# Modulation unit 4 of an adaLN hybrid layer summed on GpSimd instead of TensorE

## What is computed

```python
mod = silu(c) @ w_ada + b_ada                  # c: 1024 values, w_ada: 1024 x 3072
shift, scale, gate = split(mod, 3)
h = layer_norm(x) * (1 + scale) + shift
xa, ga, u, v, gb = split(h @ w_in, SPLITS)     # w_in: 1024 x 2560
ya = pool_mixer(xa) * silu(ga)
yb = sgu_mixer(gelu(u), gelu(v)) * silu(gb)
y = concatenate([ya, yb]) @ w_out
out = layer_norm(2**0.25 * x + gate * y) * ln_g + ln_b
```

## Time and profile before

| | |
|---|---|
| median of 3 runs | 660.97 us (660.58 to 661.17) |
| the profiled execution, its own time | 661.66 us |
| its span, first to last instruction | 659.6 us |
| TensorE products | 647.1 us busy, 98% |
| VectorE | 497.2 us, 75% |
| ScalarE | 255.7 us, 39% |
| GpSimd | 53.0 us, 8% |
| mean granted TensorE clock | 0.998 |

### The profile page before, as it was taken

How to read it: one execution, slowest core, us unless ns; L and a number is a source line. 1 busy time by engine, 2 the same in 40 slices (tenths; PEclk the granted TensorE clock), 3 DMA queues, 4 the chain that set the end, 5 groups by cost and what they waited for, 6 DMA issues and landing times.

```text
span 659.6 us, 8435 instructions
## 1 busy us (share of the span) xinstructions
PE 647.1 (98%) x3046; PEld 540.7 (82%) x3046; DVE 497.2 (75%) x981; ACT 255.7 (39%) x340; POOL 53.0 (8%) x77
## 2 busy tenths in 40 slices
PE   7999999999999999999999999999999999999995
PEld 6888888888888888888888888888888888888885
DVE  5678897887979988499959865778968845336776
ACT  4424634346512324244655323333756333323300
POOL 2000111000002230000002210000002210000010
PEclk9999999999999999999999999999999999999999
DMA  8989776989489997957658965847558886553111
GB/s 337 380 320 373 255 278 243 325 282 350 126 315 355 405 378 242 397 196 265 215 206 316 382 216 201 312 159 257 192 177 305 289 300 205 192 170 141 41 65 64
DMA packets 52170, 168.62 MB, mean 256 GB/s; under 512 B 5477, under 2 KB 9633, under 8 KB 52130
## 3 DMA queue, kind: packets, MB, share of 16 engines
q1 hardware_dynamic: 43490, 136.63, 57.3%
q10 hardware_dynamic: 8640, 31.46, 13.6%
HBM read 139.75 MB, written 28.32 MB: 255 GB/s over the span
## 4 chain that ended last, share of the span: by engine, by line
PE 95%; DVE 2%; DMA 1%; ACT 0%; issue 0%; SPq 0%; DVEq 0%; POOL 0%
PE bank_b L1374 67%; PE bank_a L1374 23%; PE bank_a L1509 2%; DMA x_norm<-in_x 1%; PE bank_a L1492 1%; DVE w_low L865 1%; DVE v_gelu L922 0%; PE bank_b L1398 0%; DVE x_stats L896 0%; PE bank_b L1434 0%; PE bank_b L1492 0%; PE bank_b L1453 0%; PE bank_b L1425 0%; ACT h_high L712 0%; DVE z L1358 0%
## 5 line engine op out<-in xcount | busy, mean ns | idle before, releaser
L1374 PE MATMUL bank_b<-h_high,w_high 128*128 128x512 f32 x512 | 202.2, 395 | 0.2 <-DVE h_low L882 0.2
L1374 PE MATMUL bank_b<-h_high,w_low 128*128 128x512 f32 x512 | 199.5, 390 | 0.0
L1374 PE MATMUL bank_b<-h_low,w_high 128*128 128x512 f32 x512 | 199.4, 389 | 0.0
L702 ACT ACTIVATE w_high<-w_float 128x1024 fp32r<-128x1024 f32 x98 | 103.1, 1055 | 111.3 <-DMA w_float<-in_w_units 71.1
L1374 PEld LDWEIGHTS bank_b<-h_high,w_high 128*128 128x128 f32 x512 | 96.2, 188 | 20.3 <-issue 0.8
L1374 PEld LDWEIGHTS bank_b<-h_high,w_low 128*128 128x128 f32 x512 | 96.1, 188 | 20.1
L1374 PEld LDWEIGHTS bank_b<-h_low,w_high 128*128 128x128 f32 x512 | 96.2, 188 | 19.3 <-issue 0.2
L638 POOL TENSOR_TENSOR z_rstd<-z_var_eps,minus_half 128x1 f32<-128x1 f32 x16 | 20.1, 1255 | 439.9 <-DVE z_var_eps L1168 229.6
L876 DVE TENSOR_TENSOR w_low<-w_float,w_high 128x1024 fp32r<-128x1024 f32 x38 | 46.3, 1220 | 8.1 <-ACT w_high L702 7.8
L1374 PE MATMUL bank_b<-w_low,y_high 128*128 128x512 f32 x96 | 37.4, 389 | 0.0
L1374 PE MATMUL bank_a<-w_high,y_low 128*128 128x512 f32 x96 | 37.4, 389 | 0.0
(11 more groups left out here) (233 smaller groups left out, 1044.0 us busy)
## 6 DMA issues: line engine op xcount, KB each, us to landing
w_float<-in_w_units SPq DMA_DIRECT2D x74, 512.0 KB, 5.2
w_low<-low_units ACTq DMA_DIRECT2D x60, 512.0 KB, 4.8
x_norm<-in_x SPq DMA_DIRECT2D x16, 512.0 KB, 7.4
low_units<-w_low SPq DMA_DIRECT2D x16, 512.0 KB, 7.5
z<-in_x SPq DMA_DIRECT2D x16, 512.0 KB, 6.4
w_float<-out_units SPq DMA_DIRECT2D x16, 512.0 KB, 4.7
out<-z SPq DMA_DIRECT2D x15, 512.0 KB, 5.3
z<-in_mod_units SPq DMA_DIRECT2D x12, 512.0 KB, 9.8
```

The source lines that it names most:

```text
L702: nc.scalar.activation(w_of(c, n)[0], w_float(c, n), ACT.Copy).then_inc(w_high, 1)
L1374: last = mm(bank, wl if n == 2 else wh, ml if n == 1 else mh, start=start and n == 0, stop=stop and n == 2, skip_group_check=skip_group_check)
```

## The change

Unit 4 leaves `PE_MODS` and gets a name of its own, `POOL_MOD`. GpSimd, after the inverse deviations of x and before the sixteen memsets, waits for silu(c) and for the landing of unit 4, multiplies its four blocks of 256 columns in place by their values of silu(c), and adds them in two steps and a third one, whose result goes into `macc`. Between dependent operations it waits on a semaphore of its own. VectorE waits for that sum before unit 5, and since the accumulator is no longer fresh, unit 5 is four accumulating operations. TensorE's `mod_own(4)` goes, and the product with ones for column 2 now starts the accumulation in the bank. SyncE loads unit 12 into the buffer once GpSimd has done, not TensorE.

```diff
--- before.py
+++ after.py
@@ -95,8 +95,9 @@
 GATE_UNITS = 8
 
 SINGLE = 4
-PE_MODS = (0, 1, 2, 4, 8)
-DVE_MODS = tuple(m for m in range(MOD_COLS) if m not in PE_MODS)
+PE_MODS = (0, 1, 2, 8)
+POOL_MOD = 4
+DVE_MODS = tuple(m for m in range(MOD_COLS) if m not in PE_MODS + (POOL_MOD,))
 
 WARM_UP = 18
 
@@ -221,6 +222,7 @@
         c_tanh, c_ready = sem("c_tanh_ready"), sem("c_ready")
         mod_multiplied, mod_used = sem("mod_unit_used_by_tensor"), sem("mod_unit_used_by_vector")
         gate_added = sem("gate_unit_added")
+        mod_pooled, pool_mod_steps = sem("mod_unit_summed_by_gpsimd"), Steps(sem("pool_mod_steps"), 0)
         mod_summed, mod_ready = sem("mod_summed"), sem("mod_ready")
         wt_turned, wt_ready = sem("wt_turned"), sem("wt_ready")
         e_done, e_ready = sem("e_done"), sem("e_ready")
@@ -487,7 +489,9 @@
             def load_m(m):
 
                 before = m - M_SLOTS
-                if before in PE_MODS:
+                if before == POOL_MOD:
+                    sp.wait_ge(mod_pooled, 1)
+                elif before in PE_MODS:
                     sp.wait_ge(mod_multiplied, PE_MODS.index(before) + 1)
                 elif before >= 0:
                     sp.wait_ge(mod_used, DVE_MODS.index(before) + 1)
@@ -648,6 +652,17 @@
                     pool.wait_ge(x_rstd, j + 1)
                     nc.gpsimd.tensor_scalar(xoff[:, j:j + 1], xmv[:, j, 0:1], xrs[:, j:j + 1], -1.0,
                                             ALU.mult, ALU.mult).then_inc(x_offset, 1)
+            pool.wait_ge(c_ready, 1)
+            m_wait(pool, POOL_MOD)
+            pool_mod_steps.begin(0)
+            rows = [m_slot(POOL_MOD)[:, a * 2 * P:(a + 1) * 2 * P] for a in range(4)]
+            for a in range(4):
+                done = nc.gpsimd.tensor_scalar(rows[a], rows[a], csilu[:, a:a + 1], None, ALU.mult)
+            pool_mod_steps.then(pool, done)
+            nc.gpsimd.tensor_tensor(rows[0], rows[0], rows[1], ALU.add)
+            pool_mod_steps.then(pool, nc.gpsimd.tensor_tensor(rows[2], rows[2], rows[3], ALU.add))
+            done = nc.gpsimd.tensor_tensor(macc[:, POOL_MOD // 4, 0:2 * P], rows[0], rows[2], ALU.add)
+            done.then_inc(mod_pooled, 1)
             for t in range(HALO):
                 nc.gpsimd.memset(count_inv[:, t:t + 1], 1.0 / (t + 1)).then_inc(const_ready, 1)
             pool.wait_ge(wsgu_landed, 16)
@@ -908,6 +923,8 @@
 
 
                 m_wait(dve, m)
+                if m == POOL_MOD + 1:
+                    dve.wait_ge(mod_pooled, 1)
                 if m < 2 * SINGLE:
                     k, fresh = m // 2, m % 2 == 0 or m - 1 in PE_MODS
                     acc, wide, first_col = macc[:, k // 2, (k % 2) * 2 * P:(k % 2 + 1) * 2 * P], 2 * P, 4 * (m % 2)
@@ -1560,7 +1577,6 @@
             early_high_passes(1)
             turn_x(2)
             early_low_pass(1).then_inc(unit_done, 1)
-            mod_own(4)
             mod_column_of(2)
             early_channel(xa, (0, 1))
             early_channel(ga, (0, 1))
```

## The result

The changed kernel takes 664.6 us (median of 4 runs, 664.19 to 665.65) against 661.07 for the kernel before beside it: a ratio of 1.0051, 95% interval 1.0038 to 1.0063, 3.4 us slower. Forecast were 661.1 and a range to 662.4. The profiled execution took 664.45 us, its span is 662.4.

A forecast was written before the change was run, and what follows sets the result against it. The prediction took VectorE's chain of waits, not TensorE's products, to bound the place. Removed products at 0 and unit 5's new form at +0.14 us made 661.66 into 661.80, or 661.1 in terms of the median; range 660.5 to 662.4.

The forecast's parts named there:

- What bounds the place: At the edit, VectorE's chain from the split at 24.40 ends TensorE's wait; TensorE idles 0.47 us until unit 5 is summed.
- The removed products at 0: TensorE's sixteen records at 25.18, about 1.75 us, lie inside its wait for unit 5, so removing them gains 0.
- Unit 5's new form, +0.14: On VectorE, four accumulating operations take 2.04 us instead of 1.90, adding 0.14 us whole to the chain of waits.
- Is GpSimd done by 25.55?: GpSimd starts unit 4 at 19.7, needs 4.3 us and is done at 24.0 (22.7 to 26.5), leaving 1.55 us of room.
- The two-input term: GpSimd's three tensor_tensor additions of unit 4, priced at 0.70 us each, between 0.40 and 1.2.
- the one-input term: GpSimd's four tensor_scalar multiplications of unit 4, priced at 0.50 us each, between 0.40 and 0.74.
- The estimate of 3.2 us: GpSimd's seven operations priced from the Trainium skill's cycles per element, without dispatch: 3.2 us, done at 22.9.
- Rival A: GpSimd late at VectorE's unit 5, 25.55, possibly held by VectorE's splits; TensorE waits too; chance 0.19 small, 0.11 large.
- its large form: GpSimd late at unit 5 with high prices and both holds: done at 28.4, VectorE 2.8 us late, total 663.9; chance 0.11.
- its small case: GpSimd late at unit 5 by up to 1.2 us: held, it ends at 26.3, VectorE waits 0.8, total 662.0; chance 0.19.
- Rival C: TensorE, idle 2.3 us before the product with ones, loses its granted clock, costing 2 us, total 663.1; chance 0.03.
- A and C as separate cases: GpSimd's lateness at unit 5 (0.19 small, 0.11 large) and TensorE's clock loss (0.03) were given separate chances.

The follow-up runs named there:

- e2_drop_only: Kernel before without TensorE's eight products of unit 4 and nothing in their place, unit 4 left out of the sum; ratio 1.0004.
- e6_sum5_first: Kernel before with one line moved: VectorE sums unit 5 before it splits early unit 4, GpSimd not used; ratio 0.9983.
- e3_beside: Kernel before, TensorE still multiplying unit 4, plus GpSimd's seven operations writing to buffers nobody reads then, VectorE not waiting for them; ratio 1.0019.
- e5_tt_form: Changed kernel with GpSimd's four tensor_scalar written as tensor_tensor with silu(c) spread over the columns; ratio 1.0016 to the kernel before.
- e9_tt_fill: Changed kernel with GpSimd's multiplications as tensor_tensor and nine idle-filling TensorE products before the product with ones; ratio 1.0008 to the kernel before.
- the second's: Profile of the unedited changed kernel run again beside the other experiments; ratio 1.0062 to the kernel before, stage +4.15 us.
- e4_two_blocks: Changed kernel with only two of unit 4's four blocks multiplied and one addition on GpSimd; ratio 1.0011 to the kernel before.
- e1_fill: Changed kernel with 17 idle-filling TensorE products where it waits for unit 5's sum; 663.27 us, ratio 1.0031 to the kernel before.

## Why the prediction was wrong, point by point

- **What bounds the place**: right. VectorE's chain, not TensorE's products, ended the wait (e2_drop_only, e6_sum5_first).
- **The removed products at 0**: right for their work (stage +0.03). The step failed in what they left behind: it said that TensorE's wait would grow to 2.3 us, and its sum has nothing for that growth.
- **Unit 5's new form, +0.14**: right; 2.04 us.
- **"Is GpSimd done by 25.55?"**: the step that failed. The two-input term (0.70) measured 0.73; the one-input term, taken at 0.50 between 0.40 and 0.74, measured 0.94 and lay outside its own range. I had built it on an affine select and a memset, which are other operations. Four times 0.44 is 1.8 us of the 2.97 by which GpSimd missed 24.0 (0.11 of it is the third multiplication's, beside the split of h); the hold behind the split of early unit 4 is 1.03, and the unit came 0.1 to 0.2 later than assumed. Without that hold GpSimd would have ended at 25.94, by this reckoning 0.4 late. The estimate of 3.2 us that stands beside the sum was further off than the sum: GpSimd took 7.1 us, 19.88 to 26.97.
- **Rival A** named the mechanism, the place and the hold, and the case happened in its large form, with 0.11. That its 663.9 is near the measured 664.6 is luck: it has GpSimd done at 28.4, which was 26.97, and nothing for the clock. (The 662.0 of its small case is 661.9 by its own terms.) Its other half, that GpSimd holds VectorE, no row showed then; e3_beside, e5_tt_form and e9_tt_fill do. The rule of the Trainium skill (SBUF — State Buffer, "Who interferes with whom"), that whichever comes first of two such instructions makes the other wait, agrees with the two-input cases among these (the product that was held in e3_beside has one input). One in the changed kernel disagrees: VectorE's two-input split of h at 21.25 came in the middle of a multiplication on GpSimd, and took the 0.69 us of the earlier trace rows:

```profile
20.79 0.93 POOL L660 TENSOR_SCALAR ln_g_rows<-ln_g_rows,c_silu 128x256 f32<-128x256 f32 x1
```

- **Rival C**, the clock, with 0.03: undervalued most. It took 1.1 us of the first profile's 2.83 and 2.4 of the second's 4.15. My evidence was the end of the trace, where the clock held through 4.5 us without a product. But the same rows show it at 0.58 within a microsecond after that, with no product left to suffer, and in e4_two_blocks it fell only once the idle time was over. So a clock of 1.00 inside an idle time is no sign that the idle time is safe, and one execution cannot show it either. By the mean clock, an idle time of 2.2 to 2.6 us lost the clock in 6 of 12, 8 of 11 and 5 of 12 runs, that of 4 us in 9 of 9.
- **A and C as separate cases**: wrong. The lateness of A lengthens the idle time on which C depends, so the likely bad case was both: 1.48 + 0.14 + the clock. The first profile's +2.83 is 1.76 for lateness and form (e1_fill) and 1.1 for the clock.

## What to carry to other kernels

Work taken off a busy engine in front of a wait of its own buys nothing, and on TensorE the gap that it leaves has a price, since the granted clock may fall about when the work comes back; look at the mean clock of every run, not only at one profile. Before moving an operation to GpSimd, measure that very operation at that size: here the form with a scalar operand was slower than the one with two tensors, and GpSimd's additions and VectorE's splits held each other when they met, in both directions. Ask first whether the engine that ends the wait has idle time earlier: moving one sum 3.4 us ahead on VectorE (e6_sum5_first) gave what the offload could not.

## What the runs showed of the hardware that I had not expected

- GpSimd's `tensor_scalar` of 256 float32 columns with a scalar from memory took 0.92 or 0.93 us where VectorE did not meet it (1.04 where it did), the same product as `tensor_tensor` with that scalar spread 0.61 (1.10 where VectorE's split met it).
- A one-input `tensor_scalar` of VectorE was held by GpSimd too: 0.82 instead of 0.35 us beside GpSimd's addition (e3_beside). VectorE's split of h, with two inputs, kept its 0.69 us beside GpSimd's `tensor_scalar` (after, 21.25), but took 0.85 beside GpSimd's `tensor_tensor` (e9_tt_fill, 21.28).
- After an idle time of about 4 us the low clock of 1.2 GHz ended at about 32.8 in one execution of the changed kernel and at about 36.1 in another, with the same waits before it. In the second it had fallen at about 29.3, before TensorE had work again at 29.93.
